# Attention value products of 64 queries each, on the two column halves of the TensorE array in turn

## What is computed

```python
kk = jnp.concatenate([jnp.pad(kb, pad)[:, :-1], kb], axis=2)      # block before, this block
vv = jnp.concatenate([jnp.pad(vb, pad)[:, :-1], vb], axis=2)
s = jnp.einsum('bnqkgd,bnskd->bnkgqs', qb, kk) * ATT_SCALE
...
p = sink_softmax(s, mask[None, :, None, None], sinks)
o = jnp.einsum('bnkgqs,bnskd->bnqkgd', p.astype(vv.dtype), vv)
```

## Time and profile before

| | us |
|---|---|
| median of 3 runs | 2479.28 (2477.75 to 2483.95) |
| span of the profiled execution | 2481.4 |
| TensorE busy in it | 2396.6 (97%) |
| VectorE, GpSimd, ScalarE busy | 1628.5, 917.9, 908.9 |
| attention stage in it | from the start to about 357 |

### The profile page before, as it was taken

The page is one execution under the profiler, slowest core; times in us unless marked ns, Lnnn a source line. Parts: engine busy times, 40 slices in busy tenths (PEclk is TensorE's granted clock), DMA queues, the critical chain, the costliest instruction groups (busy, mean ns, idle before and its releaser), DMA issues.

```text
span 2481.4 us, 36492 instructions
## 1 busy us (share of the span) xinstructions
PE 2396.6 (97%) x13782; PEld 2180.3 (88%) x13782; DVE 1628.5 (66%) x2473; ACT 908.9 (37%) x1556; POOL 917.9 (37%) x724
## 2 busy tenths in 40 slices
PE   6999989999998899999999999999999999999999
PEld 5888878999996788788888889999999899999998
DVE  4666663666667334577877786766766866766665
ACT  3444442333333123434334343333333433333232
POOL 3333211212211032563544545434444434434441
PEclk9999989999998999999999999999999999999999
DMA  7322211111114246622222362222222532222221
GB/s 262 150 89 89 76 60 58 60 63 46 55 43 134 87 158 201 219 86 86 86 85 86 98 236 69 69 70 74 66 79 71 180 133 74 67 77 69 69 68 69
DMA packets 150105, 242.85 MB, mean 98 GB/s; under 512 B 17809, under 2 KB 113773, under 8 KB 147901
## 3 DMA queue, kind: packets, MB, share of 16 engines
q1 hardware_dynamic: 149937, 240.93, 28.7%
q0 software_dynamic: 32, 0.07, 0.0%
HBM read 185.08 MB, written 56.84 MB: 97 GB/s over the span
## 4 chain that ended last, share of the span: by engine, by line
PE 56%; DVE 4%; POOL 3%; DMA 2%; issue 1%; ACT 0%; SPq 0%; POOLq 0%; ACTq 0%; DVEq 0%
PE bank L2541 10%; PE bank L2542 10%; PE bank L2543 10%; PE bank L113 8%; PE bank L115 8%; PE bank L114 8%; DMA late_b_raw<-in_w_ffn_in_dram 1%; DVE late_a_lo L2811 1%; PE bank L2484 1%; DVE late_t_lo L2819 0%; DVE late_acc L2873 0%; DVE late_gp L2847 0%; POOL late_t_raw L3008 0%; DVE late_act_lo L2829 0%; DVE late_t L2859 0%
## 5 line engine op out<-in xcount | busy, mean ns | idle before, releaser
L2847 DVE TENSOR_TENSOR late_gp<-bank,late_gp 128x384 f32<-128x384 f32 (+1 forms) x330 | 172.3, 522 | 324.7 <-PE bank L2543 324.5
L2541 PE MATMUL bank<-late_a_hi,late_b_hi 128*128 128x384 f32 (+1 forms) x1056 | 342.4, 324 | 6.3 <-DVE late_b_lo L2819 4.8
L2542 PE MATMUL bank<-late_a_lo,late_b_hi 128*128 128x384 f32 (+1 forms) x1056 | 341.3, 323 | 0.0
L2543 PE MATMUL bank<-late_a_hi,late_b_lo 128*128 128x384 f32 (+1 forms) x1056 | 340.2, 322 | 0.0
L3022 POOL TENSOR_TENSOR late_t<-late_t,late_gp 128x768 f32<-128x768 f32 (+1 forms) x66 | 132.2, 2021 | 505.1 <-DVE late_gp L2847 505.1
L113 PE MATMUL bank<-late_d_hi,late_act_hi 128*128 128x512 f32 (+1 forms) x724 | 283.7, 392 | 5.4 <-DVE late_acc L2873 3.1
L115 PE MATMUL bank<-late_d_hi,late_act_lo 128*128 128x512 f32 (+1 forms) x724 | 282.7, 390 | 0.0
L114 PE MATMUL bank<-late_d_lo,late_act_hi 128*128 128x512 f32 (+1 forms) x724 | 282.5, 390 | 0.0
L2541 PE MATMUL bank<-late_a_hi,late_t_hi 128*128 128x384 f32 (+1 forms) x792 | 259.9, 328 | 12.4 <-DVE late_gp L2847 10.8
L2873 DVE TENSOR_TENSOR late_acc<-bank,late_acc 128x512 f32<-128x512 f32 (+1 forms) x374 | 243.1, 682 | 34.8 <-PE bank L115 34.1
L2542 PE MATMUL bank<-late_a_lo,late_t_hi 128*128 128x384 f32 (+1 forms) x792 | 256.3, 324 | 0.0
(11 more groups left out here) (334 smaller groups left out, 5461.4 us busy)
## 6 DMA issues: line engine op xcount, KB each, us to landing
late_b_raw<-in_w_ffn_in_dram SPq DMA_DIRECT2D x66, 1024.0 KB, 5.1
late_d_raw<-in_w_down_dram SPq DMA_DIRECT2D x32, 1024.0 KB, 4.9
att_next_hh<-h_parts SPq DMA_DIRECT2D x16, 1024.0 KB, 4.8
late_a_raw<-h_parts SPq DMA_DIRECT2D x14, 768.0 KB, 5.4
att_x<-in_x_prompt_dram SPq DMA_DIRECT2D x16, 512.0 KB, 3.6
h_parts<-att_h_hi SPq DMA_DIRECT2D x16, 512.0 KB, 2.7
h_parts<-att_h_lo SPq DMA_DIRECT2D x16, 512.0 KB, 3.4
late_o<-mixed SPq DMA_DIRECT2D x16, 512.0 KB, 4.5
```

Of the source, the lines that this page charges most:

```text
L2541: nc.tensor.matmul(out, w_h, hi[:, c, :], start=first, stop=False, skip_group_check=True)
L2542: nc.tensor.matmul(out, w_h, lo[:, c, :], start=False, stop=False, skip_group_check=True)
L2543: ins_ = nc.tensor.matmul(out, w_l, hi[:, c, :], start=False, stop=last, skip_group_check=True)
L2847: nc.vector.tensor_tensor(dst, bk, src, ALU.add).then_inc(c_dve, 1)
```

## The change

Each value product is cut into two, for queries 0 to 63 and 64 to 127. The stationary operand becomes 128 keys x 64 queries, and the result goes to the lower or upper 64 partitions of the same PSUM columns, which places the product on the lower or upper 64 columns of the array. The moving operand is the same for both. For a head the order is: block before, lower half; block before, upper half; own block, lower half; own block, upper half. Nothing else is changed: the waits ahead of the products, the mark behind the last, and every other engine's program are as they were.

```diff
+                parts = (1,) if first else (0, 1)
                 for h in range(HQ):
                     kv = h // GQ
-                    if not first:
-                        nc.tensor.matmul(bank[3][:, h * HD:(h + 1) * HD], pT[:, h * 256:h * 256 + P],
-                                         v[:, 1 - t.p, kv * HD:(kv + 1) * HD], start=True, stop=False)
-                    ins_ = nc.tensor.matmul(bank[3][:, h * HD:(h + 1) * HD], pT[:, h * 256 + P:(h + 1) * 256],
-                                            v[:, t.p, kv * HD:(kv + 1) * HD], start=first, stop=True)
+                    for pr in parts:
+                        for half in range(2):
+                            at = h * 256 + pr * P + half * (P // 2)
+                            ins_ = nc.tensor.matmul(bank[3][half * (P // 2):(half + 1) * (P // 2), h * HD:(h + 1) * HD], pT[:, at:at + P // 2],
+                                                    v[:, t.p if pr else 1 - t.p, kv * HD:(kv + 1) * HD], start=pr == parts[0], stop=pr == 1)
                 pv.mark(ins_)
```

## The result

| | before | after |
|---|---|---|
| median, us | 2479.27 (2477.75 to 2483.95, 4 runs) | 2457.18 (2453.25 to 2458.31, 4 runs) |
| ratio | | 0.9895, 95% interval 0.9881 to 0.9909 |
| span of the profiled execution | 2481.4 | 2451.6 |
| PE busy in it | 2396.6 | 2364.9 |

Faster: by 22.1 us between the medians, and by 26.0 us by the ratio, whose interval is 22.6 to 29.5 us. The forecast was 2453.6 in 2448 to 2468.

What follows compares the result with a forecast made beforehand. TensorE, 97% busy, with the value products on the path ahead of the scores. Terms 23.5 + 0.5 - 0.1 + 1.8 = 25.7 us off 2481.4, and 2.1 lower for the median: 2453.6, range 2448 to 2462, taken to 2468.

Steps and rivals of the forecast that it cites:

- The rate of the halves: Value products on TensorE: a half product's pass takes 0.056 us, half of 0.112; a tile 1.80 us instead of 3.48.
- The two equations from L1460 and L1453: From two existing matmul groups: 7d + w = 0.45 and 3d + w = 0.23, giving step d = 0.056, first wait w = 0.06 us.
- The overlap: Value products: two column halves run side by side, a pair each 0.056 us, saving 1.68 us a tile.
- Rival 1: Value products' halves don't overlap: 3.64 us a tile, +2.4 us, about 2482 in all; chance 0.09.
- Rival 2: Each change of half empties the array in the value products: +58 us, about 2538; chance 0.05.
- Rival 3: Value products overlap only partly, about 2467, or TensorE's clock falls to half at times, 2466; chance 0.06.
- What set the 0.112 us: Distance between value-product passes before the change: read as the load of 128 columns of weights.
- The path: Attention loop: value products stand ahead of the scores, where all chains begin, so 1.68 us a tile comes through.
- the feared wait for `split_h`: Tile 0: VectorE's `split_h` runs until 59.52 with `keep_o` behind it, so the gain was put at only 0.5 us.
- The shape: Array shape change between transposes and value products: covered by the wait for `keep_p`, otherwise about 0.1 us.
- The tail: Tile 15, at the end at half clock: products would save more than 2 us; 1.8 arrives through an earlier `keep_o`.

Runs made afterwards that it cites:

- all three edits: Changed kernel plus heads 0 to 3 started early, scores alternated on two row halves, and norm sums moved before `keep_o`: median 2439.17 us, ratio 0.9828.

## Why the prediction was right

- **The rate of the halves.** The two equations from L1460 and L1453 gave 0.056 us a pass and 0.06 for the first load. Measured is 0.0585, with one half at work and with both, and 1.86 us a tile for 1.80. L1460's single starts in the kernel before already lie 0.058 to 0.059 us apart; the sum from the lengths of two groups was 4% low. The gain in a tile is 1.62 us for 1.68.
- **The overlap.** That L774's rows speak for two halves at once held; the run with one half after the other shows that the overlap is the whole gain. Rival 1 names just what that run is, a kernel almost without overlap: 3.52 us for the 3.64 worked out, with three passes side by side at the switch. Rival 2 (each change of half empties the array) is refuted by the starts, 0.024 and 0.035 us apart. Rival 3's clock stayed at 1.00.
- **What set the 0.112 us.** It was argued from the scores at 0.104 us on average. Their single starts lie 0.112 us apart too, but for three at the change of row half, which start beside another; they move twice the values, so the argument stands. The halves show it: with the load alone halved, the pass at one place falls from 0.112 to 0.0585 us.
- **The path.** The sum put 13 x 1.68 + 0.5 = 22.3 us into the stretch and 1.58 into the last distance; measured 22.5 and 1.5, together 24.0 for 23.9. Tile 0 gave 0.8 us (18.13 to 17.32 to the next tile) where 0.5 were put: the feared wait for `split_h` didn't come. That the products stand ahead of the scores was the deciding point. The same kind of cut behind the scores brings 0.4 us in the stretch, for 22.5. The 0.05 us by which the scores follow the last product sooner (147.80 - 147.65 = 0.15 for 0.20) made up for most of what the slower pass took; the prediction had counted on neither.
- **The shape.** Covered in the steady tiles by `keep_p`, where the step stays at 0.55 us. Uncovered, in tile 0, it costs 0.20 - 0.11 = 0.09 us, for 0.1.
- **The tail, right in its sum and wrong in its cause.** The prediction gave tile 15 a gain of 1.8 us, because its products end late for `keep_o`. In the profiled pair the step from the first product of tile 15 to `keep_o` is 1.88 us shorter: 356.82 - 350.41 before, 328.98 - 324.45 after. But the kernel with one half after the other, whose products of tile 15 take 3.55 us, has the same step: 354.23 - 349.69 = 4.54. Its VectorE rows, after the start of the products at 349.69:

```profile
352.55 1.76 DVE L207 TENSOR_TENSOR ahead_ml_w_lo<-ahead_ml_w_raw,att_next_hi 128x1544 fp32r<-128x1544 f32 x1
...
354.23 0.68 DVE L972 TENSOR_TENSOR att_o<-bank,att_rden 128x512 f32<-128x512 f32 x1
```

`keep_o` stands behind a split of the next stage's weights that ends at 354.3, after the products in both kernels. At full clock tile 15 brings nothing; the 1.8 us of the profiled kernel before came with the half clock of 1.2 GHz over its last products, which neither of these two traces shows there. The granted clock over the products of tile 15 in the kernel before, third from the end:

```profile
350.41:356.37 5.96, 5.96 (x39) 5.96 (x32) 4.41 (x12) 5.96 (x11) 0.00 (x0) 0.57 0.00 0
```

The clock is 1.00 there in seven of the ten traces. In the other three it is lower and the products take longer: 0.57 and 5.95 us before, 0.71 and 3.73 with four heads whole, 0.57 and 3.02 with all three edits. So it is no property of the kernel before. The prediction saw the half clock and counted it as part of the kernel. How often a launch meets it wasn't measured. It could be why the kernel with one half after the other is 0.15% faster than before (interval 0.05 to 0.24) with nearly the same stretch; that is argued, not shown.

- **The total.** 24.0 us are shown up to tile 15. The profiled spans differ by 29.8: 24.0, the tail's 1.9, 2.0 by which the first value product came earlier (57.76 to 55.77, ahead of anything changed), and some 2 of later stages, whose code is the same. The medians' 22.1 lies below 24.0 and the ratio's 26.0 (22.6 to 29.5) above it, and the forecast's 25.7 is 1.7 above it, all of it in the tail. That the profiled pair shows the tail's 1.9 is luck: one trace met the lower clock there and the other didn't. The median of the runs is 3.6 us above the forecast; 1.7 of these are the tail, and the rest is open. It is less than the later stages scatter: from `keep_o` of tile 15 to the end the ten traces have 2120 to 2128 us.

## What to carry to other kernels

Here a float32 product with a stationary operand of 128 columns and a moving one of 64 was bound by its weight load. Cut in two across the columns of the array and given out in turn, it took about half the time (1.86 us for 3.48), and cutting further took only 0.09 us more off. Before pricing a cut on the busiest engine, ask where it stands in the loop's chain: 1.6 us ahead of the scores came through whole, 1.4 us behind them became a wait, and 1 us moved on an engine that was busy for 66% took 10.0 us off the stretch, where the change took 22.5. A tail that ran at a lower clock in one profile is no term of the sum until a second trace shows it.

## What the runs showed of the hardware

- Matmuls at different column halves don't keep strictly to the order of the text in their starts: with four passes in a row at one half the other half still worked beside it (1.88 us for 64 passes); with 32 in a row three passes overlapped at the switch and no more (3.52). The scores of the kernel before show the same three at their change of row half.
- The distance of passes at one place, with 64 values to move: 0.112 us with 128 columns, 0.0585 with 64, whether the other half works or not, and 0.056 with 32.
- Weight loads overlap with matmuls that use the same rows of the array: in the change 64 loads and 64 matmuls, all on 128 rows, took 2.08 us. If a load had to wait for the matmul at its half, 32 times 0.0585 + 0.056 us would be 3.7 (an estimate from the passes above). The Trainium skill ("TensorE: Matmul & The Clock Gate", Part 3, What overlaps and what doesn't) lets loads run under matmuls only where the row groups differ, and has matmuls in strict order. The loads of this case show otherwise; for the order, the 1.88 us for the 2.8 of a strict order speak against it.
- A pass of a 64- or 32-column product that moves 64 values lasts 222 or 219 ns where that of 128 columns lasts 275.
